# A router with its weights stationary, ranks by three products, slot matrices in two halves, and first gathers indexed by VectorE, in a fused two-layer transformer kernel

## The reference, cut to what matters

```python
x = x + u @ w_out[l]
h = rmsnorm_2(x, norm2_g[l])
# hier_moe: 4 groups of 8 experts, two experts of one group for each token
g_logits = xf @ w_rg + b_rg                        # 4 columns
e_logits = (xf @ w_re + b_re).reshape(T, 4, 8)     # 32 columns
g_idx = argmax(g_logits); p_group = softmax(g_logits)[g_idx]
top_v, top_i = top_k(e_logits[g_idx], 2)
top_w = softmax(top_v) * p_group
# tokens sorted by expert into blocks of rows; each block:
y = (silu(xb @ w_gate[e]) * (xb @ w_up[e])) @ w_down[e]
# and added back to the token's row with its weight
```

## Time and profile before

| what | value |
|---|---|
| median of 3 runs | 1900.15 us (1898.16 to 1903.47) |
| profiled execution, its own time | 1900.61 us |
| its span in the trace | 1898.8 us |
| TensorE busy | 1803.0 us (95%) |
| VectorE, ScalarE, GpSimd busy | 774.5, 382.0, 110.7 us |
| chain that ended last: TensorE, VectorE, DMA, ScalarE | 93%, 3%, 1%, 1% |
| mean granted TensorE clock | 0.976 |

### The profile page before, as it was taken

How to read it: one execution, slowest core, us unless ns; L and a number is a source line. 1 busy time by engine, 2 the same in 40 slices (tenths; PEclk the granted TensorE clock), 3 DMA queues, 4 the chain that set the end, 5 groups by cost and what they waited for, 6 DMA issues and landing times.

```text
span 1898.8 us, 24374 instructions
## 1 busy us (share of the span) xinstructions
PE 1803.0 (95%) x9977; PEld 1065.3 (56%) x9977; DVE 774.5 (41%) x1574; ACT 382.0 (20%) x810; POOL 110.7 (6%) x126
## 2 busy tenths in 40 slices
PE   7999999999999999989999899977999999999993
PEld 3344555688888888545556684453444444444441
DVE  3376864464436444354434542142222222222223
ACT  3334645200000001134532320010111111111110
POOL 0000000000000000100032130000000000000002
PEclk9999999999999999989999999977999999999997
DMA  4521122221222222321111112624999999999994
GB/s 167 117 61 45 46 88 89 92 92 46 88 89 89 89 89 89 101 89 45 45 45 45 45 59 89 265 89 164 387 398 391 390 395 386 385 401 395 395 403 152
DMA packets 83826, 329.21 MB, mean 173 GB/s; under 512 B 7895, under 2 KB 9044, under 8 KB 75564
## 3 DMA queue, kind: packets, MB, share of 16 engines
q1 hardware_dynamic: 71964, 287.45, 39.8%
q0 software_dynamic: 7632, 26.11, 4.9%
q10 hardware_dynamic: 4160, 14.68, 1.9%
HBM read 305.41 MB, written 22.81 MB: 173 GB/s over the span
## 4 chain that ended last, share of the span: by engine, by line
PE 93%; DVE 3%; issue 1%; DMA 1%; ACT 1%; POOL 0%; SPq 0%; POOLq 0%; DVEq 0%; ACTq 0%
PE ps L1363 12%; PE ps L982 10%; PE ps L1026 10%; PE ps L854 8%; PE ps L1121 6%; PE ps L1371 6%; PE ps L1391 6%; PE ps L890 6%; PE ps L1268 4%; PE ps L1398 3%; PE ps L850 3%; PE ps L1306 3%; PE ps L934 2%; PE ps L1132 1%; PE ps L1353 1%; PE ps L908 1%
## 5 line engine op out<-in xcount | busy, mean ns | idle before, releaser
L1363 PE MATMUL ps<-W,yT 128*64 128x512 f32 x1024 | 228.2, 598 | 1.1 <-DVE yT L2569 1.1
L854 PE MATMUL ps<-hT,W 128*128 128x512 f32 (+1 forms) x336 | 150.5, 600 | 1.3 <-DVE hT L1852 1.3
L1363 PEld LDWEIGHTS ps<-W,yT 128*64 128x64 f32 x1024 | 71.0, 138 | 143.1 <-issue 141.7
L1121 PE MATMUL ps<-hT,W 128*128 128x512 f32 x272 | 121.5, 601 | 0.7 <-ACT gb L1629 0.7
L1371 PE MATMUL ps<-W,yT 128*32 128x256 f32 x2048 | 117.1, 381 | 0.0
L1391 PE MATMUL ps<-W,yT 128*64 128x512 f32 x512 | 116.9, 599 | 0.0
L2595 DVE COPY mix<-ps 32x256 f32<-32x256 f32 x128 | 53.9, 421 | 153.7 <-PE ps L1398 152.4
L854 PEld LDWEIGHTS ps<-hT,W 128*128 128x128 f32 (+1 forms) x336 | 61.9, 190 | 76.4 <-issue 74.5
L2576 DVE TENSOR_TENSOR yT<-yT,ps 64x512 f32<-64x512 f32 x32 | 22.1, 691 | 189.8 <-ACT yT L1784 189.8
L1371 PEld LDWEIGHTS ps<-W,yT 128*32 128x32 f32 x2048 | 63.3, 110 | 64.4 <-issue 26.0
L982 PE MATMUL ps<-yT,cbuf 128*128 128x256 f32 x384 | 85.6, 379 | 2.4 <-issue 2.4
(11 more groups left out here) (407 smaller groups left out, 2616.1 us busy)
## 6 DMA issues: line engine op xcount, KB each, us to landing
W<-in_w_expert_gate SPq DMA_DIRECT2D x32, 2048.0 KB, 15.0
W<-in_w_expert_up SPq DMA_DIRECT2D x32, 2048.0 KB, 20.0
W<-in_w_expert_down SPq DMA_DIRECT2D x32, 2048.0 KB, 20.5
W<-in_w_in SPq DMA_DIRECT2D x16, 2048.0 KB, 7.7
W<-in_w_up SPq DMA_DIRECT2D x8, 2048.0 KB, 8.2
W<-in_w_down SPq DMA_DIRECT2D x8, 2048.0 KB, 7.8
y_scratch<-mix ACTq DMA_DIRECT2D x32, 384.0 KB, 9.1
W<-in_w_out SPq DMA_DIRECT2D x4, 2048.0 KB, 7.8
```

Source lines behind the costliest of these rows:

```text
L854: ins = pe.matmul(ps[0:n, bank, :], wv[:, k, j * P:j * P + n], hT[:, k, :], start=(k == 0), stop=(k == KT - 1))
L1121: ins = pe.matmul(ps[:, bank, :], wv[:, k, j * P:(j + 1) * P], hT[:, k, :], start=(k == 0), stop=(k == KT - 1))
L1363: ins = pe.matmul(ps[64 * part:64 * part + 64, 2, :], xsT[:, x_slot, k, 0:64], wviews[s][part][:, k, :], start=(k == 0), stop=(k == KT - 1))
```

## The change

The turn of tile i follows one token tile earlier, and VectorE's loop puts the evacuation of a turn and the norm ahead of the next addition. The logits are computed with the 36 columns of router weights stationary and the 128 tokens of a tile moving, into 36 partitions; ScalarE copies them to SBUF and TensorE transposes them back. The upper half of the last turned tile is evacuated by ScalarE. Sums of the chosen-expert matrices are formed on VectorE, so that four rank products do where there were eight (one with the triangle, three with ones). The block number comes by rounding instead of a comparison with all 42 block starts, and the two matrices are made for the first choice of all tokens and then for the second, each half with its own semaphore step. VectorE writes the first two index columns itself, so GpSimd issues both gathers without a copy, and ScalarE evacuates half of the first expert's tokens.

```diff
+        lgT = smb[0:NG + NE, 1, :]
...
-            def fetch(e, s):
-                pool.tensor_copy(idcol[:, s:s + 1], idsT[:, bass.ds(e, 1)]).then_inc(idcol_ready, 1)
-                pool.wait_ge(idcol_ready, e + 1)
+            def gather_tokens(s):
                 pool.sem_inc(fetches, 1)
                 pool.indirect_dma_start(out=xs[0:BLK, s, :], out_offset=None, in_=h_dram,
                                         in_offset=bass.IndirectOffsetOnAxis(ap=idcol[:, s:s + 1], axis=0)).then_inc(gather[s], 16)
 
-            for e in range(2):
-                fetch(e, e)
+            def fetch(e, s):
+                pool.tensor_copy(idcol[:, s:s + 1], idsT[:, bass.ds(e, 1)]).then_inc(idcol_ready, 1)
+                pool.wait_ge(idcol_ready, e - 1)
+                gather_tokens(s)
+
+            for s in range(2):
+                gather_tokens(s)
+            pool.wait_ge(ids_ready, 2)
...
-                    if half == 1 and i >= 2:
-                        turn(T_N2, [i - 2])
-            turn(T_N2, [2])
+                    if half == 1 and i >= 1:
+                        turn(T_N2, [i - 1])
 
             pe.wait_ge(wr_load, 32)
             take(4, 5, 6, 7)
-            for i in range(NT):
-                if i == 2:
-                    turn(T_N2, [3])
+
+            def logits(i):
                 pe.wait_ge(turn_evac, 40 + 2 * (i + 1))
                 for k in range(KT):
-                    ins = pe.matmul(ps[:, 4, i * (NG + NE):(i + 1) * (NG + NE)], hT[:, k, i * P:(i + 1) * P],
-                                    wr[:, k, :], start=(k == 0), stop=(k == KT - 1))
-            ins.then_inc(logits_done, 1)
+                    ins = pe.matmul(ps[0:NG + NE, 5 + 2 * (i % 2), 0:P], wr[:, k, :], hT[:, k, i * P:(i + 1) * P],
+                                    start=(k == 0), stop=(k == KT - 1))
+                ins.then_inc(logits_done, 1)
+
+            def logits_back(i):
+                pe.wait_ge(route_act, i + 1)
+                return pe.transpose(ps[:, 4, i * (NG + NE):(i + 1) * (NG + NE)], lgT[:, i * P:(i + 1) * P],
+                                    ident[0:NG + NE, 0:NG + NE])
+
+            logits(0)
+            logits(1)
+            turn(T_N2, [3])
+            logits_back(0)
+            logits_back(1)
+            logits(2)
+            logits(3)
+            logits_back(2)
+            logits_back(3).then_inc(logits_done, 1)
 
             pe.wait_ge(masks_ready, 1)
...
             pe.wait_ge(sel_ready, 1)
             pe.matmul(ps[:, 5, 0:NT * NE], ltri, both_rows[:, 0:NT * NE], start=True, stop=False)
-            for d in range(1, NT):
-
-                pe.matmul(ps[:, 5, d * NE:NT * NE], allone, both_rows[:, 0:(NT - d) * NE], start=False, stop=(d == NT - 1))
-            for j in range(NT):
-                ins = pe.matmul(ps[:, 7, 0:NE], allone, msel[:, 2, j, :], start=(j == 0), stop=(j == NT - 1))
-            ins.then_inc(rank_done, 1)
-
-            pe.wait_ge(slots_ready, 1)
-            for n in range(2 * NT):
-                ins = pe.matmul(ps[0:BLK, 6, 0:BLOCKS], place_hot[:, n, :], block_tok[:, n, :],
-                                start=(n == 0), stop=(n == 2 * NT - 1))
+            pe.matmul(ps[:, 5, NE:2 * NE], allone, both_rows[:, 0:NE], start=False, stop=False)
+            pe.wait_ge(sel_ready, 2)
+            pe.matmul(ps[:, 5, 2 * NE:4 * NE], allone, sums[:, 0:2, :], start=False, stop=True)
+            pe.matmul(ps[:, 7, 0:NE], allone, sums[:, 2, :], start=True, stop=True).then_inc(rank_done, 1)
+
+            for c in range(2):
+                pe.wait_ge(slots_ready, c + 1)
+                for n in range(NT * c, NT * (c + 1)):
+                    ins = pe.matmul(ps[0:BLK, 6, 0:BLOCKS], place_hot[:, n, :], block_tok[:, n, :],
+                                    start=(n == 0), stop=(n == 2 * NT - 1))
             ins.then_inc(idT_done, 1)
-            pe.wait_ge(ids_ready, 1)
+            pe.wait_ge(ids_ready, 2)
...
+            pe.wait_ge(route_act, 7)
...
+            def logits_copy(t):
+                act.wait_ge(logits_done, t + 1)
+                act.activation(lgT[:, t * P:(t + 1) * P], ps[0:NG + NE, 5 + 2 * (t % 2), 0:P], ACT.Copy).then_inc(route_act, 1)
...
+                if a == NT - 1:
+                    for t in range(2):
+                        logits_copy(t)
+            act.wait_ge(turn_done, 48)
+            act.activation(hT[:, 4:8, 3 * P:4 * P], ps[:, turn_bank(T_N2, 3, 1), :].rearrange("p (k t) -> p k t", k=4), ACT.Copy
+                           ).then_inc(turn_evac, 1)
+            for t in range(2, NT):
+                logits_copy(t)
...
+            act.wait_ge(ex["xt"], 1)
+            act.activation(xsT[:, 0, 4:8, :], ps[:, 1, 0:4 * BLK].rearrange("p (k t) -> p k t", k=4), ACT.Copy
+                           ).then_inc(route_act, 1)
...
             for a in range(NT + 2):
+                if 0 <= a - 2:
+                    take_turned(T_N2, a - 2, range(1 if a - 2 == 3 else 2))
+                if 0 <= a - 1 < NT:
+                    norm_stage(T_N2, a - 1)
                 if a < NT:
                     add_half(1, a)
...
-            dve.wait_ge(logits_done, 1)
+            dve.wait_ge(logits_done, 5)
...
+            both = msel[:, 2, :, :]
+            dve.tensor_tensor(both, msel[:, 0, :, :], msel[:, 1, :, :], ALU.add).then_inc(sel_ready, 1)
+            dve.wait_ge(sel_ready, 1)
+            then(dve.tensor_tensor(sums[:, 0:4:3, :], both[:, 0:4:2, :], both[:, 1:4:2, :], ALU.add))
+            dve.tensor_tensor(sums[:, 1:3, :], third_and_pair, sums[:, 0:1, :].broadcast_to([P, 2, NE]), ALU.add
+                              ).then_inc(sel_ready, 1)
...
-            then(dve.tensor_tensor(r_ov, r_ov, iot[:, 0:NE], ALU.subtract))
-            then(dve.tensor_scalar(r_ov, r_ov, float(NE - 1), float(BLK), ALU.add, ALU.mult))
+            then(dve.scalar_tensor_tensor(out=r_ov, in0=r_ov, scalar=float(BLK), in1=far_base, op0=ALU.mult, op1=ALU.add))
             ranks = ps[:, 5, 0:NT * NE].rearrange("p (i e) -> p i e", i=NT)
-            over = msel[:, 2, :, :]
-            then(dve.tensor_scalar(over, ranks, float(BLK), None, ALU.is_ge))
-            then(dve.tensor_tensor(over, over, r_ov.unsqueeze(1).broadcast_to([P, NT, NE]), ALU.mult))
-            then(dve.tensor_tensor(r_rank, ranks, block_start[:, 0:NE].unsqueeze(1).broadcast_to([P, NT, NE]), ALU.add))
+            over = both
+            dve.tensor_tensor(r_rank, ranks, block_start[:, 0:NE].unsqueeze(1).broadcast_to([P, NT, NE]), ALU.add)
+            then(dve.scalar_tensor_tensor(out=over, in0=ranks, scalar=float(BLK),
+                                          in1=r_ov.unsqueeze(1).broadcast_to([P, NT, NE]), op0=ALU.is_ge, op1=ALU.mult))
             then(dve.tensor_tensor(r_rank, r_rank, over, ALU.add))
+            then(dve.tensor_tensor(r_pick, msel[:, 0:2, :, :], r_rank.unsqueeze(1).broadcast_to([P, 2, NT, NE]), ALU.mult))
+            then(dve.tensor_reduce(r_rows, r_pick, AX.X, ALU.add))
+
+            rows8 = r_rows.rearrange("p c i -> p (c i)")
+            then(dve.tensor_scalar(r_blk, rows8, 1.0 / BLK, 0.5 / BLK - 0.5, ALU.mult, ALU.add))
+            then(dve.tensor_scalar(r_blk, r_blk, ROUND, -ROUND, ALU.add, ALU.add))
+            then(dve.scalar_tensor_tensor(out=r_slot, in0=r_blk, scalar=float(-BLK), in1=rows8, op0=ALU.mult, op1=ALU.add))
             for c in range(2):
-                then(dve.tensor_tensor(r_row, msel[:, c, :, :], r_rank, ALU.mult))
-                then(dve.tensor_reduce(r_rows[:, c, :], r_row, AX.X, ALU.add))
-
-            rows8 = r_rows.rearrange("p c i -> p (c i)")
-            all_blocks = [P, 2 * NT, BLOCKS]
-            then(dve.tensor_tensor(from_block, bc(rows8, BLOCKS), block_start.unsqueeze(1).broadcast_to(all_blocks), ALU.is_ge))
-            then(dve.tensor_reduce(r_blk, from_block, AX.X, ALU.add))
-            then(dve.tensor_tensor(block_tok, bc(r_blk, BLOCKS),
-                                   iot[:, 1:BLOCKS + 1].unsqueeze(1).broadcast_to(all_blocks), ALU.is_equal))
-            for c in range(2):
-                at = block_tok[:, NT * c:NT * (c + 1), :]
+                four = slice(NT * c, NT * (c + 1))
+                at = block_tok[:, four, :]
+                then(dve.tensor_tensor(at, bc(r_blk[:, four], BLOCKS), iot[:, 0:BLOCKS].unsqueeze(1).broadcast_to([P, NT, BLOCKS]),
+                                       ALU.is_equal))
                 dve.tensor_tensor(at, at, bc(tokid[:, :], BLOCKS), ALU.mult)
-            then(dve.tensor_scalar(r_blk, r_blk, -1.0, float(-BLK), ALU.add, ALU.mult))
-            then(dve.tensor_tensor(r_blk, r_blk, rows8, ALU.add))
-            dve.tensor_tensor(place_hot, bc(r_blk, BLK), iot[:, 0:BLK].unsqueeze(1).broadcast_to([P, 2 * NT, BLK]),
-                              ALU.is_equal).then_inc(slots_ready, 1)
+                dve.tensor_tensor(place_hot[:, four, :], bc(r_slot[:, four], BLK),
```

(31 more changed lines are left out.)

9 lines of the change are left out of this document (3 added, 6 removed).

## The result

| | before | after |
|---|---|---|
| median | 1901.81 us of 4 (1898.16 to 1905.31) | 1890.72 us of 4 (1888.19 to 1896.14) |
| profiled execution, its own time | 1900.61 us | 1896.14 us |
| span | 1898.8 us | 1894.3 us |
| mean granted clock | 0.976 | 0.978 |

The ratio of the times is 0.9945 with a 95% interval of 0.992 to 0.9971: faster by 11.1 us at the median.

A forecast was written before the change was run, and what follows sets the result against it. Experts are TensorE-bound at 17.84 us each and untouched; only the 46.4 us from last projection to first expert product can shrink. 7.4 + 1.7 + 2.7 + 0.3 - 0.1 + 0.5 = 12.5 us off: median 1887.6, range 1884.5 to 1893.5.

The forecast's parts named there:

- Step 1: Last projection product to VectorE's start on the logits: 18.17 us before, 10.75 foretold, saving 7.4 us.
- Step 2: Rank products: sixteen instructions become eight, at half clock 0.215 us each, saving 1.7 us.
- Step 3: Row numbers and slot matrices: fewer, merged and halved VectorE steps save 2.7 us, between 2.0 and 3.2.
- Step 4: First gather: dropping GpSimd's copy and its hop saves 0.3 us, bounds 0 and 0.9.
- second gather beside it: Second gather, issued closer behind the first, may stretch the first's 4.11 us: 0.1 us lost, bounds 0 and 0.5.
- 5, first copies: First expert's tokens: two copies in 1.03 us become one on each of two engines, saving 0.5 us.
- The clock at the first expert: When full clock returns at the first expert's products: an unknown of 1.4 us either way.
- Rival 1: Clock falls within the logits as before; that stretch saves 2.8 us instead of 7.4, median 1892.2; chance 20%.
- Rival 2: Logits: weight load and product add up for the narrow operand, 0.22 us each; median 1894.5; chance 6%.
- Rival 3: Experts bound by DMA, later weights give back the earlier start: 1900 us, no change; chance 6%.
- Rival 4: After the experts: a near tie moves a token, an overflow block adds 37 us, median near 1925; chance 3%.

The follow-up runs named there:

- e8: The kernel before with only fills (extra products nobody reads) in TensorE's waits, nothing of the change; one execution, 1890.16 us.
- e2: The changed kernel with only the norm stage's old order of turns and VectorE loop restored, new logits form kept; one execution, 1890.20 us.
- e1: The changed kernel with only the logits' old operands restored (tokens stationary, 36 columns moving, no copies or turns back); one execution, 1893.32 us.
- e3: The changed kernel with both slot matrices made in one piece with one semaphore step, block number still by rounding; one execution, 1892.19 us.

## Why the prediction was right

The forecast was 1887.6 us; measured were 1890.72, and 1889.52 when it was repeated. Step by step, in the two profiled executions:

| step | foretold, us | measured, us | from |
|---|---|---|---|
| 1, norm to logits | 7.4 | 7.07 | 18.17 - (0.87 + 10.23) |
| 2, ranks | 1.7 | 1.70 | before 3.73 from first product to VectorE, now 1276.88 - 1274.85 |
| 3, rows and slots | 2.7 | 2.74 | before 10.59 from ranks taken to cast, now 1284.73 - 1276.88 |
| 4, gather's issue | 0.3 | 0.38 | 1.44 to 1.06 |
| 4, second gather beside it | -0.1 | 0.0 | 4.11 and 4.11 |
| 5, first copies | 0.5 | 0.42 | 2.63 to 2.21 |
| sum | 12.5 | 12.3 | 46.49 to 33.33 + 0.87 |

- *Step 1.* Its prices held: a turn 0.87, 32 logits 3.66 and 3.63 for 3.5, the last turn at 4.64 behind the product instead of 4.5. The tail and way back came to 0.70 from the last logits product to VectorE. The claim "about half is order, the rest is the clock" was unproven then. The runs take it apart, with one execution for each. Clock first: the clock alone 18.17 - 12.02 = 6.15 (`e8`, old order and old form); then the new form, which at full clock costs 13.17 - 12.02 = 1.15 for its copies and turns back (`e2`, old order); then the order, 13.17 - 11.10 = 2.07. Together 6.15 - 1.15 + 2.07 = 7.07. Order first: with the old form the order saves 18.17 - (0.87 + 13.89) = 3.41 (`e1`), and the new form then 3.66. So "half is order" holds on the second path and not on the first, since part of what the order saves is that TensorE spends less of the stretch at half clock. On both the new form is worth having only because the clock stays up with it.
- *Step 2.* The 1.70 is a saving at half clock: at full clock even the sixteen old instructions need only 1.84 us up to VectorE (`e8`, 1270.23 to 1272.07). The two new sums hid, and so did the six small weight steps, which ended at 1276.17 + 0.16, 0.55 before VectorE took the ranks.
- *Step 3.* The total is right; `e3` measures the halves by themselves at 0.8 of it. The rest is put down to fewer and merged steps; no run undoes those by themselves.
- *Step 4.* Bounds of 0 and 0.9 were kept open for what the missing copy saves; it saved 0.38, about the copy and its hop, since the 0.9 from release to transfer stayed with VectorE as the releaser. The 0.0 for the second gather is one pair of traces, and gathers differ by more than the foretold 0.1.
- *The clock at the first expert*, allowed for with 1.4 us either way, went against it: the first 32 expert products took 9.39 us where before they took 8.46, at 7.02 for full clock. That is 0.9 more lost, most of the 1.1 by which the part from the first expert to the end grew (602.05 us against 600.91).
- *The median* of both measurements lies 2 to 3 us above the forecast. The 0.2 by which the stretch fell short of the sum and the 1.1 just named are of that; the rest is no more than the level of the shared part, which differs from one execution to the next by more than that. That the whole came so near is therefore in part luck: the two comparisons of medians give 11.1 and 15.0 us for the same change. What bears the forecast out is the stretch, 12.3 and 12.1 us shorter in two traces for a foretold 12.5.

*Rival 1*, the clock falling within the logits, did not come about, though `e1` shows that it does with the old operands. The Trainium skill (TensorE: Matmul & The Clock Gate, Part 4: PE-mode transpose) has it that transposes do not count as busy in the way that products do. By themselves they did not bring the clock down here: the change has two turns and two small transposes around its first 32 logits products and PEclk is 1.00 over them, while in `e1`, with the turns in the same places, the clock fell inside products with 36 moving columns, ahead of the turn at 1259.46. *Rival 2*, load and product adding up, would have shown as 0.22 us each; it is 3.66 / 32 = 0.114. *Rival 3*, experts bound by DMA, is refuted by the 17.84 us that stayed and a single wait of TensorE there (total, times, longest):

```profile
PE ps L1404 <- DVE yT L2622: 0.4, 1, 0.4
```

*Rival 4*, the overflow block, did not come: the chain of after goes from the last expert to the store at 1867.29, with no block between.

## What to carry to other kernels

In a stretch where TensorE works in short pieces between other engines, ask first at what clock it runs there. Of two forms of a small product with the same pace, the one with more moving columns kept 2.4 GHz here, and fills in the waits gave most of the gain even to the old kernel. Fills must end before the work that they cover for is ready, at the slow clock too. A step's saving that was worked out at half clock shrinks once the clock is up. And compare a local change by the stretch that it touches, since one profiled execution can sit 8 us from the next by what happens elsewhere.

## What had not been expected of the hardware

- The clock can fall in a TensorE that never pauses: in `e1` PE is 4.00 of 4.00 us busy from 1258 to 1262 at PEclk 0.50, after 2.9 us of back-to-back products of 36 moving columns. It need not fall so soon: in `e8` it stood through 32 such products, a turn and nearly 32 more. In `e2` it stayed up through a wait of 2.9 us, with 128 moving columns behind it.
- By `e8` and after, at full clock a product of 128x128 by 36 columns and one of 128x36 by 128 columns both take 0.11 us, though one moves 3.6 times the columns of the other.
- The same first gather took 4.09 to 4.66 us in ten traces (4.11 and 4.28 in two of one kernel). The three with the old issue took 4.09, 4.11 and 4.34, the seven with the new one 4.42 in the mean, so a small effect of the closer second gather can't be excluded; half a microsecond of it in a single trace proves nothing.
- Two executions of one kernel differ by up to 10 us, by 2 us for each 0.001 of mean granted clock, and the traces show between two and six stretches at 1.2 GHz ahead of the router, some of them behind waits of TensorE that these kernels share.
